# Two attentions of a two-block transformer kernel redone: where rows are normalised, rotated, masked and gated

## The reference

```python
# first block: differential attention, 8 heads, two maps (c) of 64 channels each
h = rmsnorm(x, norm_attn_g);  u_q, u_k, u_v, u_pool, u_gate = split(h @ w_in)
q, k = rope_partial(q), rope_partial(k)       # turns 16 of the 64 rows of each map
q = q * HEAD_DIM ** -0.5
s = einsum('bqhcd,bkhcd->bhcqk', q, k)        # causal mask, blocks of 128 queries
p = softmax(where(mask, s, -inf));  w = p[:, :, 0] - lam * p[:, :, 1]
a = rmsnorm(einsum('bhqk,bkhd->bqhd', w, v), subln_g) * (1.0 - lam_init)
p = multiscale_pool(u_pool, w_pool, pool_scale)
gates = sigmoid(u_gate);  x = x + (gates[0] * a + gates[1] * p) @ w_out
# second block: stick-breaking attention, 8 heads of 64 channels, strictly causal
log_fail = where(mask, log_sigmoid(-z), 0.0)
log_later = cumsum(log_fail, reverse) - log_fail
weights = where(mask, exp(log_sigmoid(z) + log_later), 0.0)
```

## Time and profile before

| | us |
|---|---|
| median of 3 runs | 1708.85 |
| lowest and highest | 1708.67, 1712.06 |
| the profiled execution | 1707.15 |
| its span in the trace | 1705.3 |
| PE busy | 1614.6 (95% of the span) |
| DVE busy | 1001.8 (59%) |
| ACT busy | 650.5 (38%) |
| POOL busy | 256.5 (15%) |

### The profile page before, as it was taken

How to read it: one execution, slowest core, us unless ns; L and a number is a source line. 1 busy time by engine, 2 the same in 40 slices (tenths; PEclk the granted TensorE clock), 3 DMA queues, 4 the chain that set the end, 5 groups by cost and what they waited for, 6 DMA issues and landing times.

```text
span 1705.3 us, 18900 instructions
## 1 busy us (share of the span) xinstructions
PE 1614.6 (95%) x7274; PEld 1310.8 (77%) x7274; DVE 1001.8 (59%) x1394; ACT 650.5 (38%) x1044; POOL 256.5 (15%) x152
## 2 busy tenths in 40 slices
PE   7898888878999999999999999999999999999995
PEld 5776666657888888888777788789888888888884
DVE  5676777766665454535688875656565544444434
ACT  4344544445322222225455554335343322222222
POOL 2343535331100000003322001001001000000003
PEclk9998999889999999999999999999999999999998
DMA  5221211113233233322221113234322333332321
GB/s 187 65 75 50 66 53 62 53 50 120 90 100 105 92 99 99 99 87 87 90 62 63 61 63 129 82 110 146 113 74 88 99 99 99 99 99 88 100 78 68
DMA packets 45818, 151.39 MB, mean 89 GB/s; under 512 B 5536, under 2 KB 6560, under 8 KB 45600
## 3 DMA queue, kind: packets, MB, share of 16 engines
q1 hardware_dynamic: 45728, 150.18, 27.4%
HBM read 148.06 MB, written 2.10 MB: 88 GB/s over the span
## 4 chain that ended last, share of the span: by engine, by line
PE 60%; DVE 11%; ACT 4%; issue 2%; POOL 1%; DVEq 0%; ACTq 0%; POOLq 0%
PE G L698 56%; DVE WL L1442 2%; DVE T L1752 1%; DVE T L1750 1%; PE SC L698 1%; ACT WH L1058 1%; PE TP L698 1%; DVE T L1754 1%; PE O L698 1%; DVE WTl L1442 1%; DVE T L1748 1%; PE M L698 1%; DVE XGl L1443 1%; ACT X L1058 0%; DVE MGl L1442 0%
## 5 line engine op out<-in xcount | busy, mean ns | idle before, releaser
L698 PE MATMUL G<-XGh,WH 128*128 128x512 f32 x1248 | 507.0, 406 | 16.3 <-DVE T L1554 15.4
L698 PE MATMUL G<-XGl,WH 128*128 128x512 f32 x1248 | 493.4, 395 | 0.0
L698 PE MATMUL G<-XGh,WL 128*128 128x512 f32 x1248 | 493.0, 395 | 0.0
L1442 DVE TENSOR_TENSOR WL<-RAW,WH 128x1024 fp32r<-128x1024 f32 (+1 forms) x232 | 284.0, 1225 | 133.9 <-ACT WH L1058 133.5
L1058 ACT ACTIVATE WH<-RAW 128x1024 fp32r<-128x1024 f32 (+2 forms) x284 | 286.0, 1009 | 182.7 <-PE G L698 171.3
L698 PEld LDWEIGHTS G<-XGh,WH 128*128 128x128 f32 x1248 | 239.2, 192 | 79.8 <-DVE T L1554 17.0
L698 PEld LDWEIGHTS G<-XGh,WL 128*128 128x128 f32 x1248 | 238.6, 191 | 51.9
L698 PEld LDWEIGHTS G<-XGl,WH 128*128 128x128 f32 x1248 | 239.1, 192 | 49.2 <-issue 2.2
L698 PE MATMUL G<-MGh,WH 128*128 128x512 f32 x436 | 171.5, 393 | 3.2 <-ACT MGh L1058 1.9
L698 PE MATMUL G<-MGl,WH 128*128 128x512 f32 x436 | 170.4, 391 | 1.3 <-DVE MGl L1442 1.3
L698 PE MATMUL G<-MGh,WL 128*128 128x512 f32 x436 | 169.9, 390 | 0.0
(11 more groups left out here) (296 smaller groups left out, 2010.4 us busy)
## 6 DMA issues: line engine op xcount, KB each, us to landing
RAW<-in_up SPq DMA_DIRECT2D x32, 512.0 KB, 3.5
RAW<-in_dn SPq DMA_DIRECT2D x32, 512.0 KB, 3.5
RAW<-in_fg SPq DMA_DIRECT2D x22, 512.0 KB, 3.5
RAW<-in_fu SPq DMA_DIRECT2D x22, 512.0 KB, 3.5
RAW<-in_g SPq DMA_DIRECT2D x16, 512.0 KB, 3.5
RAW<-in_f SPq DMA_DIRECT2D x16, 512.0 KB, 3.5
X<-in_x SPq DMA_DIRECT2D x16, 256.0 KB, 4.6
RAW<-in_va SPq DMA_DIRECT2D x8, 512.0 KB, 4.5
```

What stands on the lines that cost most here:

```text
L698: return e.matmul(dst, st, mv, start=start, stop=stop, skip_group_check=True)
L1442: return e.tensor_tensor(dst, src, hi.bitcast(F32), ALU.subtract)
```

## The change

First attention. The input is multiplied once by gain and root (new steps "x_mul" and "x_lo", on DVE, ACT and DVE, eight of each, laid between the last matmuls of v), so that no bank of q, k, pool or gate has to be multiplied by RB. Banks of q and k are emptied by ACT into QKh and by DVE into QKl. The columns of w_q and w_k are put in another order on the host, so that the 32 rows to be turned of a unit lie together (rows 48 to 79); for two heads at a time four transfers bring these rows, high and low, from the QK tile into T ("rot_in"), DVE, POOL and ACT turn them as one tile of 128 rows ("rot_mix", "rot_add"), and four transfers take them back. The QK tile holds four heads in place of two. One DVE instruction per map adds the mask to the scores, writes the sum to SBUF and gives the row's minimum of the negated sum, and the exponential reads SBUF. Gates leave PSUM on ACT as tanh(u/2), with the halves put into the gains, and DVE does the joins (three of its instructions become five, two of POOL's fall away). The table of tanh also holds the exponential. Low parts of q, k, pool and wp weights move from POOL to DVE. The order of units and steps is a list (HEADS_A): the attention begins after 14 of the 72 ticks, and its 32 score blocks follow at 1.8 ticks each.

Second attention. DVE adds the mask in PSUM, ACT makes sigmoid(-z) and sigmoid(z), DVE takes a running product backwards and multiplies it in; the turn comes three ticks after the scores.

The scratch for software descriptors is set to 256 bytes. The diff, cut to what matters:

```diff
-ON_POOL = ("q", "k", "g0", "g1", "pool", "wp", "qb", "kb", "ub")
-
...
+TABLES = {ACT.Exp: ("exp_and_others", "natural_log_exp_and_others"), ACT.Tanh: ("exp_and_others",),
+          ACT.Ln: ("natural_log_exp_and_others",), ACT.Sigmoid: ("sigmoid_and_others",), ACT.Sin: ("trig_and_small",),
+          ACT.Silu: ("silu_and_others",)}
...
+HEADS_A = [("qk", 0), ("qk", 1), ("pool", 0), ("gate", 0), ("wp", 0), ("qk", 2), ("qk", 3), ("pool", 1), ("qk", 4),
+           ("gate", 1), ("qk", 5), ("wp", 1), ("gate", 2), ("pool", 2), ("qk", 6), ("qk", 7), ("gate", 3), ("gate", 4),
+           ("wp", 2), ("pool", 3), ("gate", 5), ("gate", 6), ("wp", 3), ("gate", 7)]
+FIRST_A, PACE_A = 5, 1.8
...
-        self.v_gemm("va", 1, 4, {(0, 2): [("cols", "attn"), *(("vev", "va", 0, m) for m in range(4))],
-                                 (1, 3): [("rotation",)]})
+        between = {(0, 2): [("cols", "attn"), *(("vev", "va", 0, m) for m in range(4))]}
+        for k in range(9):
+            at = between.setdefault((1 + k // 4, k % 4), [])
+            if k < 8:
+                at.append(("x_mul", k))
+            if k > 0:
+                at.append(("x_lo", k - 1))
...
+    def attention_a(self, start):
+
+        done = {}
+        for s in range(32):
+            h, i = s // 4, s % 4
+            o = start + int(s * PACE_A) - self.clock
+            self.later(o, "scores_a", h, i)
+            self.later(o + 1, "weights_a", h, i)
+            self.later(o + 3, "turn_a", h, i)
+            if i == 3:
+                self.later(o + 4, "pv_a", h)
+                self.later(o + 5, "post_a", h)
+                done[h] = self.clock + o + 5
+        return done
+
+    def merge_a(self, h, at):
+        self.later(at - self.clock, "mix_a", h)
+        self.later(at + 1 - self.clock, "sum_a", h)
...
+                    self.gemm("qk"[w], i, ("qk", i, w))
+                    self.put("qk", i, w)
+                if i % 2 == 1:
+                    self.later(0, "rot_in", i // 2)
+                    self.later(2, "rot_mix", i // 2)
+                    self.later(3, "rot_add", i // 2)
...
+                elif kind == "rot_in":
+                    p = arg[0]
...
+                    for j in range(4):
+                        sl = slot(2 * p + j // 2, j % 2)
+                        e.dma_start(T[32 * j:32 * j + 32, 0:2, :], QK[ROT, :, sl, :].bitcast(F32)).then_inc(d_rin, 16)
...
+                    e.wait_ge(r_lo, p + 1)
...
+                        e.dma_start(QK[ROT, :, sl, :].bitcast(F32), T[32 * j:32 * j + 32, 1:3, :]).then_inc(d_rout, 16)
...
                     qs = slice(i * P, (i + 1) * P)
...
-                                e.wait_ge(sa_exp, 2 * SA[step] - 3 + c)
+                                e.wait_ge(sa_max, 2 * SA[step] - 3 + c)
...
+                elif kind == "qk":
+                    h, w = arg
+                    e.wait_ge(unit_done, gemm_done(step))
+                    if h >= 4:
+                        e.wait_ge(sa_done, 2 * SA["scores_a", h - 4, 3])
...
+                    e.wait_ge(unit_done, gemm_done(step))
+                    if h > 0:
+                        e.wait_ge(mg_lo if w == 0 else mr_done, MRG["sum_a", h - 1])
+                    else:
+                        e.wait_ge(xn_lo, 8)
+                    e.activation(gate_of(h, w), G[:, turn_of[step] % 2, :], ACT.Tanh, scale=0.5).then_inc(g_moved, 1)
...
-                    e.wait_ge(sa_max, SA[step])
-                    if s >= 1:
-                        e.wait_ge(wa_inv, s)
+                    if s >= 2:
+                        e.wait_ge(wa_inv, s - 1)
                     for c in range(2):
-                        if c == 0 and s >= 3:
-                            e.wait_ge(turned, s - 2)
-                        if c == 1 and s >= 2:
-                            e.wait_ge(wa_done, s - 1)
-                        dst = (T[:, 3 + s % 3, 0:n], T[:, 6 + s % 2, 0:n])[c]
-                        e.activation(dst, SC[:, c, 0:n], ACT.Exp, bias=NM[:, c:c + 1],
-                                     accum_out=LS[:, c:c + 1]).then_inc(sa_exp, 1)
+                        j = 2 * (s % 2) + c
+                        e.wait_ge(sa_max, 2 * s + c + 1)
+                        e.activation(weight_of(s, c), weight_of(s, c), ACT.Exp, bias=NM[:, j:j + 1], scale=-1.0,
+                                     accum_out=LS[:, j:j + 1]).then_inc(sa_exp, 1)
 
...
                         e.wait_ge(eps_set, 1)
-                    e.activation(SQ, M[:, :], ACT.Ln, bias=EPSC, scale=SUB ** -2 / P).then_inc(ss_ln, 1)
+                    e.wait_ge(ss_done, POST[step])
+                    e.activation(rs, M[:, :], ACT.Ln, bias=EPSC).then_inc(ss_ln, 1)
                     e.wait_ge(ss_ln, POST[step])
-                    e.activation(SQ, SQ, ACT.Exp, scale=-0.5).then_inc(ss_root, 1)
-
...
+                elif kind == "weights_b":
                     h, i = arg
...
+                    elif s >= 2:
+                        e.wait_ge(wb_done, s - 1)
+                    e.wait_ge(sb_masked, s + 1)
+                    e.activation(fail, z, ACT.Sigmoid, scale=-1.0).then_inc(sb_fail, 1)
+                    if s >= 5:
                         e.wait_ge(turned, TURN["turn_b", (s - 5) // 4, (s - 5) % 4])
-                    e.wait_ge(sb_done, s + 1)
-                    e.activation(R, z, ACT.Abs).then_inc(sb_abs, 1)
-                    e.wait_ge(sb_abs, s + 1)
-                    e.activation(R, R, ACT.Exp, scale=-1.0).then_inc(sb_exp, 1)
-                    e.wait_ge(sb_exp, s + 1)
-                    e.activation(R, R, ACT.Ln, bias=1.0).then_inc(sb_ln, 1)
...
+                    e.activation(W_, z, ACT.Sigmoid).then_inc(sb_win, 1)
...
+                elif kind == "x_mul":
...
+                    e.scalar_tensor_tensor(X[:, k, :], X[:, k, :], gain(G_ATTN, k), RB[:, :], ALU.mult,
+                                           ALU.mult).then_inc(xn_mul, 1)
+
+                elif kind == "x_lo":
+                    k = arg[0]
+                    e.wait_ge(xn_hi, k + 1)
+                    lo(XGl[:, k, :], X[:, k, :], XGh[:, k, :]).then_inc(xn_lo, 1)
...
-                elif kind == "rope":
+                elif kind == "qk":
                     h, w = arg
...
-                    e.scalar_tensor_tensor(qa, G[:, turn_of[step] % 2, :], HEAD ** -0.5 if w == 0 else 1.0, RB[:, :],
-                                           ALU.mult, ALU.mult).then_inc(g_empty, 1)
-                    e.wait_ge(g_empty, EMPTY[step])
-                    e.stream_shuffle(qb, qa, SHUF).then_inc(qb_shuf, 1)
-                    e.wait_ge(qb_shuf, ROPE[step])
-                    e.tensor_tensor(qb, qb, SIN, ALU.mult).then_inc(qb_sin, 1)
+                    g = G[:, turn_of[step] % 2, :]
+                    e.wait_ge(qk_hi, QKN[step])
+                    lo(QKl[:, slot(h, w), :], g, QKh[:, slot(h, w), :], HEAD ** -0.5 if w == 0 else None).then_inc(
+                        g_empty, 1)
+
+                elif kind == "rot_mix":
+                    p = arg[0]
+                    qa, qb = T[:, 0, :], T[:, 2, :]
+                    e.wait_ge(d_rin, 64 * (p + 1))
+                    e.tensor_tensor(qa, qa, T[:, 1, :], ALU.add).then_inc(r_raw, 1)
+                    e.wait_ge(r_raw, p + 1)
+                    if p > 0:
+                        e.wait_ge(d_rout, 64 * p)
+                    e.stream_shuffle(qb, qa, SHUF).then_inc(r_shuf, 1)
+                    e.wait_ge(r_shuf, p + 1)
+                    e.tensor_tensor(qb, qb, SIN, ALU.mult).then_inc(r_sin, 1)
...
                     h, i = arg
-                    n = (i + 1) * P
-                    dg = SC[:, :, i * P:n]
-                    if (h, i) == (0, 0):
+                    s, n = 4 * h + i, (i + 1) * P
+                    if s == 0:
                         e.wait_ge(d_mask, 16)
-                    e.wait_ge(sa_done, 2 * SA[step])
-                    e.tensor_tensor(dg, dg, MSK[:, :, :], ALU.add).then_inc(sa_masked, 1)
-                    e.wait_ge(sa_masked, SA[step])
-                    e.tensor_reduce(NM[:, 0:2], SC[:, :, 0:n], AX, ALU.max, negate=True).then_inc(sa_max, 1)
+                    if s >= 2:
+                        e.wait_ge(sa_exp, 2 * (s - 1))
+                    for c in range(2):
+                        j = 2 * (s % 2) + c
+                        if c == 0 and s >= 3:
+                            e.wait_ge(turned, s - 2)
+                        if c == 1 and s >= 2:
+                            e.wait_ge(wa_done, s - 1)
+                        e.wait_ge(sa_done, 2 * s + c + 1)
+                        e.tensor_tensor_reduce(weight_of(s, c), SC[:, c, 0:n], MSK[:, S - n:S], -1.0, 3.0e38, ALU.add,
+                                               ALU.min, NM[:, j:j + 1]).then_inc(sa_max, 1)
...
-                    e.tensor_tensor(RL[:, 1:2], RL[:, 1:2], NLAM, ALU.mult).then_inc(wa_lam, 1)
-                    e.wait_ge(wa_lam, s + 1)
```

(48 more changed lines are left out.)

419 lines of the change are left out of this document (215 added, 204 removed).

## The result

The changed kernel takes 1664.65 us (median of 4 runs, 1662.28 to 1665.76) against 1708.76 (4 runs, 1708.39 to 1712.06): a ratio of 0.9736, 95% interval 0.9719 to 0.9753, 44 us less. The forecast was 1643, its range 1622 to 1672; the range of its main case, 1628 to 1660, was missed by 5 us. The profiled execution of the changed kernel took 1665.76 us (span 1664.0), 41.4 less than the one of before; 22.6 us of the 64 that the sum held are missing, and what follows looks for them.

What follows compares the result with a forecast made beforehand. The prediction took the kernel to be PE-bound, losing most in the first attention behind DVE's full queue. Savings of 38 (idling), 23 (clock) and 3 (second attention), 64 us, from 1707.15 gave 1643 us, range 1622 to 1672.

Steps and rivals of the forecast that it cites:

- main case: Whole kernel: the forecast of 1643 us with its own range 1628 to 1660, chance 0.7.
- Idling, 38 of 52 forecast: First attention: of 52 us of PE idling 14 would be left, so 38 saved.
- The entry: Start of the first attention: new DVE work under thin cover, new PE waits of 2.9 and 2.7 us, 5.6 in all.
- in the later pairs: covered: First attention, later pairs of heads: six or seven ticks of over 4 us cover the transfers of turned rows.
- The transfers: First attention, turned rows: four land in 3.5 to 5 us; as rival, 14 per set gives 1698; slower than before, chance 0.03.
- The clock, 23 forecast: First attention: 28 us lost to the low clock, 5 of it to stay, so 23 saved.
- the same matmuls would take 272: First attention: with idling and clock loss both gone, PE's matmuls would take 272 us.
- the rival at 1621: Both attentions: all waits go, 52 + 28 + 6 = 86 us saved, 1621 us; chance 0.05.
- Second attention, 3 saved forecast: Second attention: fewer DVE and ACT instructions per block save 3 of the 6 us it can give.
- the earlier turn costs nothing: Second attention: the work before the turn is under 5 us and three ticks are over 8, so no cost.
- DVE's work: First attention: DVE busy time falls from 248 to 186 us, 156 going and 94 coming.
- The first rival: First attention: waits move to DVE at post_a and ACT at gemm ends; half the loss stays, 1667 us; chance 0.2.

Runs made afterwards that it cites:

- The experiment: Turn of the second attention's last weights four ticks behind the scores instead of three, against the changed kernel: 1655.70 us, ratio 0.9684.

## Why the prediction came out as it did

The direction, the place and the mechanism held; the size was some 22 us too large. By the terms of the sum:

- **Idling, 38 of 52 forecast, 30.5 measured.** Left were 21.7 us, not 14. The entry cost less than the 5.6 us kept for it: a wait of 2.2 us at 62.0 (2.9 forecast); the second, 2.7 at 74, is 0.6 us in the changed kernel and 1.7, at 75 us, in seven of the twelve experiments. The 4.2 us at 158 is where "in the later pairs: covered" failed. The transfers themselves were cheap, as forecast: each lands 2.4 us after its issue, and SP needs 2.5 to 2.9 us to issue four. But the ticks of cover were spent before them, on waiting for the mixing's place in the order and in DVE's queue. The other waits for the masking reduction took 4.8 us where 1 was kept for the score banks, and the row sums 3.1, for which no term stood by name. The transposed weights took 4.1 us where 3 were kept for them and for the pooled rows, which had 1.2.
- **The clock, 23 forecast, 15.1 measured.** This is the step that failed most in its working. The clock column was multiplied by the length of the window, but the low level lies partly over time in which PE idles anyway, so 0.08 x 352.5 = 28 counts some of the 52 us of idling again. The trace before has 58.0 us at the low level in this window, PE is busy in 47.8 of them, and half of that, 23.9, is what it cost; the changed kernel has 17.1, all under a busy PE, and so 8.5. Taken from 300.3 and 285.2, both leave 276 to 277 us for the same matmuls, so "the same matmuls would take 272" was some 4 us too low, and with it the rival at 1621 too low by as much. The loss left was 8.5 us where the forecast kept 5: more waits stayed than it saw.
- **Second attention, 3 saved forecast, 3.4 lost** (the offset of the same matmul falls from 45.7 to 42.3). Of the 3.4, 1.6 are the low clock at 770 us, ahead of the second attention and of anything that the change touched there; the other 1.8 are the second attention's own, 178.1 us for 176.3, with 1.7 of low clock behind the new wait. The step that failed is "the earlier turn costs nothing". Its arithmetic was of the work between scores and turn; what it left out is what the turn stands in front of in DVE's queue. The experiment shows it to be worth 8.4 us in the second attention: 6.5 of idling, and slow matmuls behind. And 22 us less of DVE work did nothing for waits that were set by that order.
- **The rest, 1.0 lost** between 1647 us and the end. It is the last pair of matmuls, which runs at the low clock in the changed kernel and ran at the high one before:

```profile
1689.60 1.10 PE L854 MATMUL M<-F,ONE 128*128 128x512 f32 x2 [2.83 <-issue]
```

```profile
1647.29 2.05 PE L918 MATMUL M<-F,ONE 128*128 128x512 f32 x2 [2.82 <-issue]
```

In both kernels PE idles 2.8 us ahead of the pair; the low level begins at 1691.1 us before and at 1647.1 in the changed kernel. No term stood for it; nothing of the change touches this pair, and why the clock fell earlier beside it stays open.

Together: 7.5 + 7.9 + 6.4 + 1.0 = 22.8, for the 22.6 that are missing.

**DVE's work** came out at 194.7 us against 186. The masking reduction was sized right (0.484 us in the mean where 0.49 was forecast; with the reads it covers 28.9 us for 31), and at 684 ns for 512 columns beside 692 for an addition of that size it takes no second pass. The row sums were taken as they were before, slowed by POOL; alone they would be 12.7 us shorter, so the collisions that stayed are more than the whole excess.

**The first rival** said that waits at post_a would take the place. DVE does wait there, 21.4 us, and it costs nothing measurable. The rival's time, 1667, lies nearest the measured one, yet not by this mechanism; its second half, ACT held at the end of each gemm, wasn't tested. **The transfers** as a rival were wrong in their price: a set of four took at most 4.3 us (154.0 to 158.3), not 14.

**What bought the gain.** Undoing the rotation costs 29.4 us and undoing the masking reduction 12.6. That makes 42 of the 44 us, but both were never undone together, so they need not add up. The load is shown as a cause by the two kernels with idle reductions: at this point 1 us of DVE work costs 0.8 us. By that rate, the rotation's 38 us of load would be worth 31, all of its 29.4; no kernel kept its chain of five instructions without their load, so this share is worked out and not shown. The rate isn't a law either: with the gates' low parts on DVE its busy time rose by 4.0 us and the time didn't. For the reduction, 11.2 us of load would be worth 9 of 12.6, so there the share of the banks' earlier release, which the name of the wait speaks for, is argued and not separated. The normalisation done once, the evictions by ACT and the gates by tanh weren't undone one by one.

## What to carry to other kernels

Before moving a step in an in-order schedule, list what comes to stand behind it on every engine, not only what lies between it and its consumer: a wait on an engine with room, put in front of urgent work in the queue, cost 8.4 us here. Read the cost of a low clock from PE's busy time, since the clock column over a window can count idling twice (28 us for 23.9 here). When PE waits for an engine that has room, as DVE did here at 63 to 70% busy, a kernel with idle instructions measures what its load costs. And look at what an instruction takes beside its neighbour before handing work over: 27 us of low parts given to POOL took 2.3 us off DVE's busy time here.

## What the runs showed that was not expected

- Work handed from POOL to DVE didn't make the kernel slower: of 20.7 us of new work on DVE its row sums gave back 12.7, and the stretch became 4.0 us shorter, 1.0 of it idling. A TENSOR_SCALAR of 512 columns takes 547 ns alone and 1.24 us in the mean of the changed kernel, where some of them meet a low part on POOL of 2.5 us.
- The masking reduction with a maximum out of PSUM takes 684, 550, 418 and 283 ns for 512, 384, 256 and 128 columns, as much as an addition of the same size, and a read of 82 ns for its accumulator.
- A wait for several things can change its name and keep its length: 4.0 to 4.2 us at 158 us were put down to the reductions in two kernels and to the returned rows in four others.
